# A scan's block inverse: a level works on 32 of 64 columns instead of all

## The chip, the cores and the metric

The kernel runs on one core of one Trainium2 chip. The metric is the device time of one execution in microseconds (us); lower is better. A change is judged by the median of several runs beside runs of the kernel before.

## The reference, cut to what matters

The program is four transformer layers in sequence (two of one model, two of another), 256 tokens by 1024 channels in f32. The second layer mixes tokens by a recurrence over time for each of 16 heads of 64 channels:

```
def step(state, inp):
    r_t, w_t, k_t, v_t, a_t, b_t = inp
    sa = jnp.einsum('bhij,bhj->bhi', state, a_t)
    state = (state * w_t[:, :, None, :] + sa[..., None] * b_t[:, :, None, :]
             + v_t[..., None] * k_t[:, :, None, :])
    y_t = jnp.einsum('bhij,bhj->bhi', state, r_t)
    return state, y_t
```

All else in the layers (feed-forward nets, attentions, norms) is not touched by the change.

## The kernel before

The recurrence is computed in chunks of 64 tokens. Within a chunk the terms `sa` depend on one another through a strictly triangular 64x64 matrix L, so that each head and chunk needs the inverse of a unit triangular matrix. It is built by doubling. At level lv the matrix consists of diagonal blocks of b = 2^lv tokens whose inverses are already there; two neighbouring blocks make a pair, and the level fills in the corner that joins them: (inverse of one) x (corner of L) x (inverse of the other). Levels 1 to 5 take b from 2 to 32 up to the whole 64.

A tile of 128 tokens is t (0 or 1). It holds two chunks (e = 0, 1), which lie on the two halves of the partitions. The 16 heads are two groups o (0, 1) of eight, each group four pairs r of two heads x. So `sY[o]` is [128, 4, 2, 64]: partitions (e, token), then r, x, and 64 columns. There are 2 tiles x 2 groups x 5 levels = 20 level steps, and each of them is this work:

- `level_a` on TensorE: four transposes of `sY` (L2311, called X below), and sixteen 64x64 products W = L x Y (L2317), on the four quarters of the array in turn (`UNITS`).
- ScalarE copies the transposes from PSUM to `sX` (L2446); VectorE copies W from PSUM to `sW` (L2504, 512 columns).
- `level_b` on TensorE: sixteen 64x64 products Y = X x W (L2328). It waits for both copies.
- VectorE writes the new corner into `sY` by a copy under a mask (L2510, 512 columns); the mask `rMK[:, 4 + lv, :]` is bf16, read as uint16 and repeated over r and x. The next level's transposes wait for it.

Each f32 product shows as two MATMUL and two LDWEIGHTS records in the trace, so the 320 products of L2317 and of L2328 are 640 records each.

The order of the work is written out by hand in `scan_steps()`, and every engine follows that one list, each in its own queue. For t = 0 a level is: level_a of o = 0, level_a of o = 1, a small product `scl` (L2259, levels 1 to 4), level_b of o = 0, level_b of o = 1, then `complete` (levels 0 to 4), which is work for the other tile: up to level 2 only on VectorE, from level 3 also on TensorE (L1785), ScalarE and VectorE (L2094 to L2099). At levels 4 and 5 `tt` (transposes L2270 for the other tile, with a copy L2497) follows. For t = 1 a level is the two level_a and the two level_b, and beside them: `state` (L2376, L2385) after level 1, `yo` (L2400 to L2412) after level 2, and pieces of `norm`, a normalisation of the scan's output on VectorE with a part on ScalarE (L2474) and on GpSimd (L964, L966): its first three pieces after level 3, the rest of that half and three of the next after level 4, the rest after level 5. What follows the scan is the layer's output product (L490 to L492) and a norm.

Of the kernel before, what the change touches and what calls it, by code (L numbers as in the profile page):

```python
# [7 lines left out]
F32 = mybir.dt.float32  # L8
# [6 lines left out]
P = 128  # L15
# [12 lines left out]
HD = 64  # L28
# [212 lines left out]
class Net:  # L241


    def __init__(self, nc, A, out, ctx, stages):
# [6 lines left out]
        def at(name, offset, shape, dt):  # L251
            return nc.alloc_sbuf_tensor_at(name, shape, dt, offset=BASE + offset)

        o = 0
# [16 lines left out]
        XO = o  # L271
# [67 lines left out]
        self.TT01 = [at(f"sTA{t}", (TO + 8192, EO + 24576)[t], [P, 8, 2, P], F32) for t in range(T)]  # L339
        self.TT23 = [at(f"sTB{o}", XO + 4096 * o, [P, 4, 2, P], F32) for o in range(2)]  # L340
        self.sX = [at(f"sXX{o}", XO + 8192 + 4096 * o, [P, 4, P], F32) for o in range(2)]
        self.sW = [at(f"sWW{o}", XO + 10240 + 4096 * o, [P, 2, 4, HD], F32) for o in range(2)]
        self.KR0 = [at(f"sKR{o}", XO + 8192 + 4096 * o, [P, 4, 2, HD], F32) for o in range(2)]
        self.KR1 = [[at(f"sKQ{t}{o}", spot, [P, 4, 2, HD], F32) for o, spot in enumerate(spots)] for t, spots in
                    enumerate(((second + 4096, second + 6144), (AO + 4096, JO)))]
# [1959 lines left out]
    def pe_scan_level_a(self, pe, t, o, lv):  # L2305
        L, Y = self.sL[o], self.sY[o]
        bank, _ = self.scan_pair(pe, ("x", t, o, lv), (self.moved, "x", t, o, lv))
        pe.wait_ge(self.made, "y", t, o, lv - 1)
        pe.wait_ge(self.made, "l", t, o)
        for r in range(4):  # L2310
            m = pe.e.transpose(bank[:, r * P:(r + 1) * P], Y[:, r, :, :].rearrange("p x n -> p (x n)"), self.ident[:, :])  # L2311
        m.then_inc(*self.product.up("x", t, o, lv))
        banks = self.scan_pair(pe, ("w", t, o, lv), (self.made, "w", t, o, lv))
        for r in range(4):
            for e, x in self.UNITS:
                h = self.HALF[e]
                m = pe.e.matmul(banks[e][self.HALF[x], r * HD:(r + 1) * HD], L[h, r, x, :], Y[h, r, x, :], start=True,  # L2317
                                stop=True)
        m.then_inc(*self.product.up("w", t, o, lv))

    def pe_scan_level_b(self, pe, t, o, lv):
        banks = self.scan_pair(pe, ("y", t, o, lv), (self.made, "y", t, o, lv))
        pe.wait_ge(self.moved, "x", t, o, lv)
        pe.wait_ge(self.made, "w", t, o, lv)
        for r in range(4):
            for e, x in self.UNITS:
                h = self.HALF[x]
                m = pe.e.matmul(banks[x][self.HALF[e], r * HD:(r + 1) * HD], self.sX[o][h, r, e * HD:(e + 1) * HD],  # L2328
                                self.sW[o][h, e, r, :], start=True, stop=True)
        m.then_inc(*self.product.up("y", t, o, lv))  # L2330

# [159 lines left out]
    def dve_rwkv_scan(self, dve, n):  # L2491
        dve.wait_ge(self.d_one["masks"])
        for kind, *a in self.scan_steps() + list(self.SCAN_TAIL):
            if kind == "tt":
                t, o = a
                dve.wait_ge(self.product, "tt", t, o, 1)
                dve.e.tensor_copy(self.TT23[o][:, :, :, :].rearrange("p r i n -> p i r n"), self.scan_banks(  # L2497
                    "tt", t, o, 1).rearrange("p (i r n) -> p i r n", i=2, r=4)).then_inc(*self.made.up("tt", t, o))
            elif kind == "gram":
                self.dve_scan_gram(dve, *a)  # L2500
            elif kind == "level_a":
                t, o, lv = a
                dve.wait_ge(self.product, "w", t, o, lv)
                dve.e.tensor_copy(self.sW[o][:, :, :, :], self.scan_banks("w", t, o, lv).rearrange(  # L2504
                    "p (e c) -> p e c", e=2)[:, :, 0:256].rearrange("p e (r n) -> p e r n", r=4)).then_inc(
                    *self.made.up("w", t, o, lv))
            elif kind == "level_b":
                t, o, lv = a
                dve.wait_ge(self.product, "y", t, o, lv)
                dve.e.copy_predicated(self.sY[o][:, :, :, :].rearrange("p r x n -> p x r n"), self.scan_mask(4 + lv, True),  # L2510
                                      self.scan_banks("y", t, o, lv).rearrange("p (x c) -> p x c", x=2)[
                                          :, :, 0:256].rearrange("p x (r n) -> p x r n", r=4)).then_inc(
                    *self.made.up("y", t, o, lv))
            elif kind == "seen":
                c, = a
                t, h = c // 2, self.HALF[c % 2]
                for o in range(2):
                    x = self.sA[t][h, 4 * o:4 * o + 4, :, :].rearrange("p r x n -> p x r n")
                    banks = self.scan_banks("seen", c, 0 if c == 3 else o)
                    dve.wait_ge(self.product, "seen", c, 1 if c == 3 else o)  # L2520
                    dve.wait_ge(self.moved, "sa0", t, o, 1)
                    dve.e.tensor_tensor(x, banks[h, :].rearrange("p (x r n) -> p x r n", x=2, r=8)[
                        :, :, 4 * o:4 * o + 4, :], x, ALU.add).then_inc(*self.made.up("sa", c, o))
            elif kind == "state":
                self.dve_scan_state(dve, *a)
            elif kind == "complete":
                self.dve_scan_complete(dve, *a)
            elif kind == "norm":
                t, h, first, end = a
                for seg in range(first, end):  # L2530
                    self.dve_scan_norm(dve, t, h, seg)
            elif kind == "turn":
                t, q = a
                hi, lo = (x[:, 4 * q:4 * q + 4, t * P:(t + 1) * P] for x in (self.XH, self.XL))
                dve.wait_ge(self.moved, "ro", t, q)
                dve.e.tensor_tensor(lo, self.bank(self.place["turn", ("ro", t, q)]).rearrange("p (k s) -> p k s", k=4),
                                    hi.bitcast(F32), ALU.subtract).then_inc(*self.made.up("ro", t, q))
        self.dve_out(dve, n)

    def scan_mask(self, i, bits=False):  # L2540
        m = self.rMK[:, i, :].bitcast(mybir.dt.uint16) if bits else self.rMK[:, i, :]
        return m.unsqueeze(1).unsqueeze(1).broadcast_to([P, 2, 4, HD])
# [238 lines left out]
```

## Time and profile before

| | |
|---|---|
| three timed runs | 2408.38, 2408.85, 2411.97 us; median 2408.85 |
| the profiled execution | 2401.35 us, of which the span is 2399.5 us |
| TensorE busy in the span | 2278.4 us (95%) |
| VectorE busy | 1493.5 us (62%) |
| ScalarE busy | 1158.4 us (48%) |
| mean granted TensorE clock | 0.983 |

PE is TensorE's matmuls, PEld its weight loads, DVE VectorE, ACT ScalarE, POOL GpSimd. The profiled execution was 7.5 us faster than the median of the timed ones, so durations are taken from its trace and differences are set against the median. The levels of the scan lie between 911.5 and 993 us of the span.

### The profile page before, as it was taken

The numbers are of one execution on the slowest core, as the hardware profiler recorded it, in microseconds if no ns is written. First come the engines' busy times: TensorE is split into PE (matmuls) and PEld (weight loads), VectorE is DVE, ScalarE is ACT, GpSimd is POOL, SyncE is SP. The second block draws the span as 40 slices with busy tenths as digits, with TensorE's granted clock in tenths as the row PEclk, the third lists the DMA queues.
The fourth block names the chain that finished last, engine by engine and source line by source line (L and its number), as shares of the span: only waits on it lengthen the run. The fifth ranks groups of instructions, "written<-read, shape, count | busy, mean of one in ns | idle before, by whom it ended". The sixth has DMA issues, their size and how long they took to land.

```text
span 2399.5 us, 32778 instructions
## 1 busy us (share of the span) xinstructions
PE 2278.4 (95%) x12883; PEld 1840.0 (77%) x12883; DVE 1493.5 (62%) x2069; ACT 1158.4 (48%) x1672; POOL 175.0 (7%) x288
## 2 busy tenths in 40 slices
PE   8999999999998988889999999998999999969998
PEld 6888778887887557768887888866888788748886
DVE  5656657647665867576557656655655765647655
ACT  5445545446544453244455445444445544545444
POOL 1001000001000010410011000001000000041001
PEclk9999999999999999989999999999999999989999
DMA  7556636554646420056555655513555555506552
GB/s 243 191 182 216 216 122 220 180 192 156 213 165 213 156 99 4 21 179 193 177 200 167 192 185 197 178 36 116 188 184 193 176 186 185 194 10 205 177 184 105
DMA packets 289751, 395.68 MB, mean 165 GB/s; under 512 B 11672, under 2 KB 193248, under 8 KB 289600
## 3 DMA queue, kind: packets, MB, share of 16 engines
q1 hardware_dynamic: 284800, 377.33, 47.4%
q0 software_dynamic: 4656, 16.20, 2.0%
q8 instruction: 104, 1.70, 0.3%
q14 instruction: 47, 0.39, 0.0%
q10 hardware_dynamic: 144, 0.07, 0.0%
HBM read 392.50 MB, written 1.05 MB: 164 GB/s over the span
## 4 chain that ended last, share of the span: by engine, by line
PE 75%; DVE 6%; ACT 4%; issue 2%; POOL 1%; DMA 0%; DVEq 0%; POOLq 0%; ACTq 0%; SPq 0%
PE bank L490 22%; PE bank L492 22%; PE bank L491 22%; PE bank L516 1%; PE bank L1320 1%; ACT wh L605 1%; PE bank L504 1%; ACT JUNK L612 1%; DVE wl L789 1%; DVE TMP L827 1%; DVE qPS L1677 0%; DVE H L847 0%; PE bank L1322 0%; PE bank L1347 0%; PE bank L1334 0%
## 5 line engine op out<-in xcount | busy, mean ns | idle before, releaser
L789 DVE TENSOR_TENSOR wl<-raw,wh 128x1024 fp32r<-128x1024 f32 x708 | 859.4, 1224 | 592.0 <-ACT wh L605 591.1
L605 ACT ACTIVATE wh<-raw 128x1024 fp32r<-128x1024 f32 x708 | 743.9, 1058 | 671.3 <-PE bank L492 641.7
L490 PE MATMUL bank<-wh,XH 128*128 128x512 f32 x2000 | 802.6, 401 | 26.8 <-DVE XL L806 6.1
L491 PE MATMUL bank<-wl,XH 128*128 128x512 f32 x2000 | 784.5, 392 | 0.0
L492 PE MATMUL bank<-wh,XL 128*128 128x512 f32 x2000 | 784.3, 392 | 0.0
L490 PEld LDWEIGHTS bank<-wh,XH 128*128 128x128 f32 x2000 | 379.1, 190 | 116.2 <-issue 20.5
L492 PEld LDWEIGHTS bank<-wh,XL 128*128 128x128 f32 x2000 | 378.6, 189 | 82.2
L491 PEld LDWEIGHTS bank<-wl,XH 128*128 128x128 f32 x2000 | 379.7, 190 | 74.4 <-issue 0.5
L490 PE MATMUL bank<-wh,AH 128*128 128x512 f32 x704 | 276.0, 392 | 0.0
L492 PE MATMUL bank<-wh,AL 128*128 128x512 f32 x704 | 274.1, 389 | 0.0
L491 PE MATMUL bank<-wl,AH 128*128 128x512 f32 x704 | 274.1, 389 | 0.0
L492 PEld LDWEIGHTS bank<-wh,AL 128*128 128x128 f32 x704 | 132.1, 188 | 27.9
L491 PEld LDWEIGHTS bank<-wl,AH 128*128 128x128 f32 x704 | 132.2, 188 | 26.8
L490 PEld LDWEIGHTS bank<-wh,AH 128*128 128x128 f32 x704 | 132.2, 188 | 26.6
L987 POOL TENSOR_SCALAR ST<-ST 128x1 f32<-128x1 f32 x32 | 8.3, 259 | 1359.2 <-ACT JUNK L612 1358.8
L702 ACT ACTIVATE AH<-bank 128x512 fp32r<-128x512 f32 x88 | 52.7, 599 | 111.8 <-PE bank L516 111.6
L891 DVE TENSOR_TENSOR AL<-bank,AH 128x512 fp32r<-128x512 f32 x88 | 60.8, 691 | 56.4 <-ACT AH L702 56.4
L921 DVE SCALAR_TENSOR_TENSOR att<-att,ST,bank 128x256 f32<-128x256 f32 x176 | 84.7, 481 | 6.2
L617 ACT ACTIVATE XH<-CT 128x512 fp32r<-128x512 f32 x60 | 37.3, 629 | 101.6 <-DVE CT L800 101.6
L732 ACT ACTIVATE att<-bank,ST 128x256 f32<-128x256 f32 x176 | 72.3, 462 | 12.7 <-POOL ST L1020 12.7
L918 DVE SCALAR_TENSOR_TENSOR att<-att,bank 128x256 f32<-128x256 f32 x176 | 72.9, 414 | 5.2 <-ACT att L732 5.2
L847 DVE SCALAR_TENSOR_TENSOR H<-TMP,ST,H 128x512 f32<-128x512 f32 x64 | 45.3, 749 | 24.5 <-POOL ST L991 24.5
(317 smaller groups left out, 1771.0 us busy)
## 6 DMA issues: line engine op xcount, KB each, us to landing
raw<-in_ffn_w_dram SPq DMA_DIRECT2D x184, 512.0 KB, 4.6
raw<-in_ffn_wi_dram SPq DMA_DIRECT2D x176, 512.0 KB, 4.6
raw<-in_ffn_w_dram SPq DMA_DIRECT2D x40, 1024.0 KB, 4.9
raw<-in_ffn_wo_dram SPq DMA_DIRECT2D x40, 1024.0 KB, 4.9
raw<-in_a_wqkv_dram SPq DMA_DIRECT2D x18, 1024.0 KB, 4.8
raw<-in_a_w_in_dram SPq DMA_DIRECT2D x16, 1024.0 KB, 5.7
raw<-in_b_w_in_dram SPq DMA_DIRECT2D x12, 1024.0 KB, 4.9
bc<-in_norm_g_dram POOLq DMA_DIRECT2D x16, 512.0 KB, 5.4
```

What stands on the lines that cost most here:

```text
L490: pe.e.matmul(o, a, h, start=(k == 0), stop=False)
L491: pe.e.matmul(o, a, l, start=False, stop=False)
L492: m = pe.e.matmul(o, b, h, start=False, stop=(k == layer.nk - 1))
L605: act.e.activation(self.wh[j % N_W][:, 0:p.size], self.raw[p.chunk % N_RAW][:, p.at:p.at + p.size], ACT.Copy).then_inc(*self.rounded.up(j))
L617: act.e.activation(self.XH[:, 4 * b:4 * b + 4, t * P:(t + 1) * P], self.CT[b][:, :, :], ACT.Copy).then_inc(*self.x_hi.up(n, t, b))
L702: act.e.activation(self.AH[:, 2 * b:2 * b + 2, :], bank.rearrange("p (k s) -> p k s", k=2), ACT.Copy).then_inc(*self.hid_hi.up(n, b))
L732: act.e.activation(self.att[b % 3][:, t * FB:(t + 1) * FB], self.pair((n, "up", b))[t][:, 0:FB], ACT.Tanh, scale=sc[:, t:t + 1]).then_inc( ...
L789: dve.e.tensor_tensor(self.wl[j % N_W][:, 0:p.size], self.raw[p.chunk % N_RAW][:, p.at:p.at + p.size], self.wh[j % N_W][:, 0:p.size].bitca ...
L847: dve.e.scalar_tensor_tensor(part, self.TMP[:, t, b, 512:1024], x, part, ALU.mult, ALU.add).then_inc(*self.resid.up(n, t, b))
L891: dve.e.tensor_tensor(lo, bank.rearrange("p (k s) -> p k s", k=2), hi.bitcast(F32), ALU.subtract).then_inc(*self.hid_lo.up(n, b))
L918: dve.e.scalar_tensor_tensor(x, x, 1.0, pair[:, 0:FB], ALU.add, ALU.mult).then_inc(*self.gate.up(n, b, t))
L921: dve.e.scalar_tensor_tensor(x, x, sc[:, T + t:T + t + 1], pair[:, FB:2 * FB], ALU.mult, ALU.mult).then_inc(*self.gated.up(n, b, t))
```

## The change

For a level only the second block of each pair has new columns: 32 of the 64 columns of each head, at every level. The kernel after multiplies and moves only those.

- W: the product's moving side is the second blocks' columns of Y, picked by a strided view (`scan_right`, runs of b columns every 2b); the result is 32 packed columns a unit.
- The copy of W to `sW` moves 256 columns in place of 512.
- Y = X x W has 32 moving columns in place of 64. The weights (`sX`, `L`) and their loads stay at 64 columns.
- The copy under the mask moves 2 x 128 columns in place of 512. It becomes two instructions, one for each x, with a view of `sY` in runs of b columns; only the second of them signals.

```
-        self.sW = [at(f"sWW{o}", XO + 10240 + 4096 * o, [P, 2, 4, HD], F32) for o in range(2)]
+        self.sW = [at(f"sWW{o}", XO + 10240 + 4096 * o, [P, 2, 4, 32], F32) for o in range(2)]
...
-                m = pe.e.matmul(banks[e][self.HALF[x], r * HD:(r + 1) * HD], L[h, r, x, :], Y[h, r, x, :], start=True,
-                                stop=True)
+                m = pe.e.matmul(banks[e][self.HALF[x], r * 32:(r + 1) * 32].rearrange("p (g b) -> p g b", b=2 ** lv),
+                                L[h, r, x, :], self.scan_right(Y[h, r, x, :], lv), start=True, stop=True)
...
-                m = pe.e.matmul(banks[x][self.HALF[e], r * HD:(r + 1) * HD], self.sX[o][h, r, e * HD:(e + 1) * HD],
+                m = pe.e.matmul(banks[x][self.HALF[e], r * 32:(r + 1) * 32], self.sX[o][h, r, e * HD:(e + 1) * HD],
                                 self.sW[o][h, e, r, :], start=True, stop=True)
...
-                dve.e.tensor_copy(self.sW[o][:, :, :, :], self.scan_banks("w", t, o, lv).rearrange(
-                    "p (e c) -> p e c", e=2)[:, :, 0:256].rearrange("p e (r n) -> p e r n", r=4)).then_inc(
-                    *self.made.up("w", t, o, lv))
+                dve.e.tensor_copy(self.sW[o][:, :, :, :].rearrange("p e r n -> p e (r n)"), self.scan_banks(
+                    "w", t, o, lv).rearrange("p (e c) -> p e c", e=2)[:, :, 0:128]).then_inc(*self.made.up("w", t, o, lv))
...
-                dve.e.copy_predicated(self.sY[o][:, :, :, :].rearrange("p r x n -> p x r n"), self.scan_mask(4 + lv, True),
-                                      self.scan_banks("y", t, o, lv).rearrange("p (x c) -> p x c", x=2)[
-                                          :, :, 0:256].rearrange("p x (r n) -> p x r n", r=4)).then_inc(
-                    *self.made.up("y", t, o, lv))
+                b = 2 ** lv
+                mask = self.scan_right(self.rMK[:, 4 + lv, :].bitcast(mybir.dt.uint16), lv)
+                for x in range(2):
+                    m = dve.e.copy_predicated(
+                        self.sY[o][:, :, x, :].rearrange("p r (g i b) -> p r g i b", i=2, b=b)[:, :, :, 1, :],
+                        mask.unsqueeze(1).broadcast_to([P, 4, 32 // b, b]),
+                        self.scan_banks("y", t, o, lv)[:, x * 512:x * 512 + 128].rearrange("p (r g b) -> p r g b", r=4, b=b))
+                m.then_inc(*self.made.up("y", t, o, lv))
...
+    def scan_right(self, x, lv):
+
+        return x.rearrange("p (g i b) -> p g i b", i=2, b=2 ** lv)[:, :, 1, :]
```

## Rows read from the trace of the kernel before

**Rows 1.** The page's first part: busy time, share of the span, instructions.

```profile
PE 2278.4 (95%) x12883; PEld 1840.0 (77%) x12883; DVE 1493.5 (62%) x2069; ACT 1158.4 (48%) x1672; POOL 175.0 (7%) x288
```

**Rows 2.** Busy time by stretch: both tiles' levels; granted clock, DMA share, GB/s last.

```profile
911.50:938.00 26.50, 25.68 (x660) 20.77 (x659) 22.47 (x34) 11.59 (x23) 0.00 (x0) 1.00 0.01 3
...
956.00:992.00 36.00, 26.47 (x906) 23.27 (x904) 21.71 (x36) 8.15 (x15) 11.64 (x10) 0.93 0.01 3
```

**Rows 3.** Groups by line and shape: busy us, mean ns, idle before and its releaser.

```profile
L2510 DVE COPY_PREDICATED sYY<-rMK,bank 128x512 f32<-128x512 uint16 x20 | 14.1, 728 | 4.1 <-PE bank L2328 3.9
L2317 PE MATMUL bank<-sYY,sLL 64*64 64x64 f32 x640 | 13.9, 224 | 0.1
...
L2328 PE MATMUL bank<-sWW,sXX 64*64 64x64 f32 x640 | 13.5, 231 | 9.4 <-DVE sWW L2504 9.4
L2504 DVE COPY sWW<-bank 128x512 f32<-128x512 f32 x20 | 13.3, 685 | 7.9 <-PE bank L2317 7.8
```

**Rows 4.** Timeline, level 2 of tile 0: start, duration, engine, line, idle and releaser.

```profile
916.52 0.66 PE L2311 MATMUL bank<-ident,sYY 128*128 128x128 f32 x4 [0.39 <-DVE sYY L2510]
...
918.95 1.05 PE L2259 MATMUL bank<-rCU,rLW 128*128 128x2 f32 x8
...
919.02 1.28 DVE L2504 COPY sWW<-bank 128x512 f32<-128x512 f32 x2
...
919.93 1.21 PE L2328 MATMUL bank<-sWW,sXX 64*64 64x64 f32 x64
...
920.69 1.34 DVE L2510 COPY_PREDICATED sYY<-rMK,bank 128x512 f32<-128x512 uint16 x2 [0.39 <-PE bank L2328]
...
921.48 0.66 PE L2311 MATMUL bank<-ident,sYY 128*128 128x128 f32 x4 [0.34 <-DVE sYY L2510]
```

**Rows 5.** Timeline: group 1 at level 5 of tile 0, level 1 of tile 1.

```profile
938.53 0.69 DVE L2504 COPY sWW<-bank 128x512 f32<-128x512 f32 x1 [0.22 <-PE bank L2317]
...
958.57 0.69 DVE L2504 COPY sWW<-bank 128x512 f32<-128x512 f32 x1 [0.52 <-PE bank L2317]
...
959.40 0.69 PE L2328 MATMUL bank<-sWW,sXX 64*64 64x64 f32 x32 [0.44 <-DVE sWW L2504]
```

**Rows 6.** Timeline, tile 1: end of level 3, level 4, and level 5.

```profile
976.00 0.74 DVE L2510 COPY_PREDICATED sYY<-rMK,bank 128x512 f32<-128x512 uint16 x1 [0.26 <-PE bank L2328]
...
979.61 1.28 DVE L2504 COPY sWW<-bank 128x512 f32<-128x512 f32 x2
...
980.43 1.29 PE L2328 MATMUL bank<-sWW,sXX 64*64 64x64 f32 x64 [2.07 <-DVE sWW L2504]
981.19 1.34 DVE L2510 COPY_PREDICATED sYY<-rMK,bank 128x512 f32<-128x512 uint16 x2 [0.30 <-PE bank L2328]
...
982.43 0.67 DVE L2619 TENSOR_REDUCE rSM<-rK 128x8 f32<-128x512 f32 x1
...
990.31 1.98 PE L2328 MATMUL bank<-sWW,sXX 64*64 64x64 f32 x64 [5.85 <-DVE sWW L2504]
```

**Rows 7.** VectorE work of other sizes: ns min/median/max.

```profile
L1267 DVE TENSOR_TENSOR dTR<-TMP,dRP x48: 216/219/226, 1478.2 to 1535.0; 128x64 f32<-128x64 f32 x48
...
L2577 DVE TENSOR_TENSOR sSS<-bank,sSS x4: 410/420/424, 962.0 to 1002.6; 128x256 f32<-128x256 f32 x4
```

**Rows 8.** Products of other widths: durations (ns min/median/max), then two runs of them.

```profile
L2317 PE MATMUL bank<-sYY,sLL x640: 218/218/268, 912.2 to 984.2; 64*64 64x64 f32 x160
...
L2290 PE MATMUL bank<-sTA,sTB x256: 269/269/418, 898.2 to 952.5; 64*64 64x128 f32 x128
...
L2259 PE MATMUL bank<-rCU,rLW x32: 251/251/272, 914.0 to 931.0; 128*128 128x2 f32 x32
...
907.39 1.96 PE L2290 MATMUL bank<-sTA,sTB 64*64 64x128 f32 x64
...
917.11 0.69 PE L2317 MATMUL bank<-sYY,sLL 64*64 64x64 f32 x32
```

**Rows 9.** Two single microseconds: busy time of each engine, clock, DMA.

```profile
979.00:980.00 1.00, 0.00 (x0) 0.00 (x0) 1.00 (x2) 0.86 (x2) 0.00 (x0) 1.00 0.00 0
...
988.00:989.00 1.00, 0.00 (x0) 0.00 (x0) 0.23 (x2) 0.86 (x2) 0.00 (x0) 0.50 0.00 0
```

## The prediction

> **What bounds the kernel now.** I read the page first. TensorE is busy 95% of the span and no other engine over 62% [rows 1], so for the kernel as a whole the products are the bound. That average says nothing of the scan, which is a different stage, so the next view was busy time by stretch. While the levels of tile 0 run, TensorE is nearly full (25.68 of 26.5 us); while those of tile 1 run it has 26.47 of 36 us, so something else sets a quarter of that time. DMA share is 0.01 in both: no transfer matters here [rows 2]. The groups by line then give the most that the change could touch: 13.9 + 13.5 us of products, 13.3 us of copies of W and 14.1 us of copies under the mask, all told 55 us, or 2% of the span. Their idle columns say which of it is waited for: TensorE sat idle 9.4 us for the copy of W [rows 3], and how much of that belongs to the copy itself has to be read in the order of time. The chain of waits and the timeline of each level show three kinds of level:
>
> - Tile 0, levels 1 and 2: TensorE runs X, W, X, W, `scl`, Y, Y without a break, then X of the next level stands idle 0.39 and 0.34 us for the copy under the mask of group 0. The copy of W is hidden: it begins at 919.02 and takes 0.69 us, and Y begins only at 919.93, when `scl` leaves TensorE [rows 4]. At levels 3 and 4 TensorE goes on with other products after Y, and nothing waits for either copy.
> - Tile 0 level 5 and tile 1 levels 1 to 3: nothing stands between W and Y of group 1. The copy of W of group 1 starts as W ends and Y starts as the copy ends (958.57 + 0.69, then 959.40) [rows 5].
> - Tile 1 from the end of level 3: VectorE is the chain. Copy under the mask, norm pieces, both copies of W, (Y on TensorE), both copies under the mask, next norm piece at once [rows 6]. TensorE waits 2.07 us there and 5.85 us at level 5.
>
> So the change shortens a chain in 2 + 4 levels and in the two and a bit at the end; in the other places of the 20 steps it shortens work that nobody waits for.
>
> **The products.** Half the moving columns does not mean half the time. 64 records of 128 columns span 1.96 us, (1.96 - 0.27) / 63 = 27 ns apart; with four quarters in turn, that is 107 ns a quarter. 32 records of 64 columns span 0.69: (0.69 - 0.22) / 31 = 15.2 ns, 61 ns a quarter, not the 54 that half of 107 would be. The records of `scl` have only 2 moving columns but 128 columns of weights: 8 in 1.05 us, (1.05 - 0.25) / 7 = 114 ns apart [rows 4, 8]. So spacing there is the weight load's; half of 114 for 64 columns of weights is 57, which is what the 61 nearly is. The change leaves the weights at 64 columns. I therefore take the spacing as unchanged, and count only the last record's own duration: 269 ns at 128 columns and 218 at 64, 51 less for 64 columns [rows 8], so 26 ns less for 32. Bounds: nothing, if a strided read costs what the skipped columns would; and spacing halved to 7.6 ns, 31 x 7.6 = 0.24 us a group of 32, if the stream is what counts after all.
>
> The Trainium skill, "TensorE: Matmul & The Clock Gate", section "LDWEIGHTS (loading the stationary operand)", says that a weight load takes its column count over 1.2 GHz, whatever the rows; the same page's "Back-to-back issue gap" gives a stream of moving columns at 2.4 GHz. By the first 64 columns of weights are 53 ns and no product gets shorter, by the second alone each would, which is the rival priced below.
>
> **The copy of W.** 512 columns take 685 ns [rows 3]; no copy of 256 stands in this stretch, but a VectorE operation from PSUM on 256 takes 420 [rows 7]. That is 265 less, 1.03 ns a column. On the line through both, 64 columns would take 221, and the trace has 219 for 64, in runs of eight columns at that [rows 7], so the fixed part is 155 and short runs cost nothing extra there. I take 0.265 us off each copy.
>
> **The copy under the mask.** One of 512 takes 728 ns; two in a row take 1.34 us, so the second starts 0.61 after the first [rows 3, 4], and they overlap by 0.12. One of 128 columns is then 728 - 384 x 1.03 = 0.33 us. The pair, with the same overlap, is 0.21 + 0.33 = 0.54 in place of 0.73: 0.19 us off. No row shows a copy under a mask of this size or with runs of 2 columns. Bounds: each of the two as long as the one before, +0.61 us; or only 0.07 off, if they don't overlap at all. The value I take lies by the line of rows 7, which holds down to 64 columns.
>
> The rule that speaks against this part is in the Trainium skill, "VectorE: DVE Perf Modes", section "The TRN2 errata — SBUF-src ops pay a fixed extra latency per instruction": the fixed cost comes once per instruction, and operations under 512 elements are to be avoided. By its fitted form (N + 151) / 0.96 the pair in sequence is 0.58 us, and the sum below would be 0.2 us smaller.
>
> **The sum.**
> - Tile 0, levels 1 and 2: 0.19 for the pair + 0.026 for Y, twice: 0.43. TensorE's idle of 0.34 or more covers it [rows 4].
> - Tile 0 level 5, tile 1 levels 1 to 3: 0.265 + 0.026 for the end of W, four times: 1.16.
> - End of tile 1's level 3: norm starts after the second pair, 0.19 + 0.026 sooner: 0.22.
> - Levels 4 and 5 of tile 1: the first copy of W 0.265, Y 0.026, the second pair 0.19; the second copy of W is off the path, since Y of group 1 comes 0.6 us after Y of group 0; and the second pair can't start sooner than its product, so the first pair's gain goes there. 0.48, twice: 0.96.
>
> Together 2.8 us. Levels 1 to 4 of the copies in tile 0, and levels 3 and 4 of its masks, are at nothing: `scl` and L1785 hide them, and the slack only grows, as VectorE gets some 9 us of the 27.4 us of these copies back (20 x 0.265 + 20 x 0.19). Nothing after the scan has a due time of its own (DMA 0.01, raw weights long there), so what the scan gives is passed on. The execution of this trace would be 2401.35 - 2.8 = 2398.6; set against the median of the timed runs, 2408.85 - 2.8 = 2406.0. That is 0.12%, under the 0.2% (4.8 us) that a measurement of this kernel can tell from no change.
>
> **Rivals.**
> - *The stream counts.* The products do take half. Some 30 groups of 32 records stand on TensorE's chain (all in tile 0 but the covered ones, about 17; three a level in levels 1 to 3 of tile 1; a few after): 30 x 0.24 = 7.3 us more, 2398.7. For it: 61 is not 57. Against it: 114 ns with two moving columns.
> - *The clock falls.* Slower. Half as many columns pass through the array in the same time. TensorE's clock is granted by what it did: after stretches without a product at 979 to 980 it was still at full (2.4 GHz), after the longer idle from 984.5 on it was at 0.50 (1.2 GHz) by 988, and the two Y groups that ran there took 1.98 us in place of 1.29 [rows 6, 9], 26 ns apart in place of 15. If the sparser products in tile 0's levels count as idleness, the 14 us of them that are groups of W and Y grow by that factor of 1.7, 9.8 us: 2415.8. It decides from 4 us of such work at the lower clock, which eat up the 2.8. Against it: `scl` with 2 columns runs at full clock now, and the spacing of instructions stays. (The page on TensorE, section "What's actually happening", has activity release the throttle; it doesn't say that half-wide products fail to.)
> - *The short pair is dear.* If runs of 2 to 16 columns or the second instruction cost what a full one does, +0.61 in place of -0.19 at the seven places where a pair stands in a chain (two in tile 0, one, two, two in tile 1), of which the sum has five: 7 x 0.61 = 4.3, less the copies' 1.6: 2411.5.
> - *It is hidden.* Another wait ends last in the chains (ScalarE's `sX`, the small GpSimd steps): 2408.5.
>
> **How the numbers follow.** The forecast 0.62; stream 0.12; clock 0.10; dear pair 0.08; hidden 0.08. Of the forecast's cases 0.10 are measured faster by over 0.2%, since it is over half way there and the timed runs alone differ by 3.6 us; 0.02 slower. Faster: 0.10 + 0.12 = 0.22. Slower: 0.02 + 0.08 of the clock + 0.03 of the pair = 0.13. Same: 0.65. The range goes from the stream rival, 2399, to somewhat over the dear pair, 2413, and leaves the deep clock case out. The forecast's own range is 2403 to 2409.
>
> **What the profile after would show.** L2504 on 256 columns at 0.42 us; L2510 x40 at 0.33, pairs 0.54 long; L2317 and L2328 with 32 columns, 192 ns each, a group still 0.67 long; idle before X at level 2 of tile 0 down to about 0.2; Y of tile 1's level 1 0.29 sooner after W; clock as before. Groups of 32 products in 0.45 us would prove the stream rival, a granted clock under 1 between 911 and 985 the clock rival, a pair over 0.73 us the dear one.

## The result

The changed kernel is a little faster: 2404.66 us median of 20 runs (2398.92 to 2411.9), the kernel before 2411.26 us (2403.49 to 2416.49, 20 runs). The ratio is 0.9976 with a 95% interval of 0.9966 to 0.9985, so 5.8 us less (3.6 to 8.2); the ratio is not that of the two medians, which lie 6.6 us apart. Later sessions gave the same kernel 0.9980 (0.9961 to 0.9999) and 0.9982 (0.9968 to 0.9997). The forecast was 2.8 us less, called "same", and the range 2399 to 2413. The median lies in the range; the timed size is larger than forecast and, in this first session, just on the other side of the line of 0.2%. The sign holds, and so does where the time was gained; one term of the sum had the wrong cause (below, the products).

The profiled execution after took 2406.57 us, that of before 2401.35. Single executions scatter by more than the effect, so a comparison of the two spans would say "slower". What the change did has to be read in the stage it touches.

The groups by line, of the kernel after (L2510 became L2512):

```profile
L2317 PE MATMUL bank<-sYY,sLL 64*64 64x32 f32 x640 | 13.4, 222 | 0.1
...
L2328 PE MATMUL bank<-sWW,sXX 64*64 64x32 f32 x640 | 12.9, 227 | 7.8 <-DVE sWW L2504 7.8
...
L2512 DVE COPY_PREDICATED sYY<-rMK,bank 128x128 f32<-128x128 uint16 x40 | 10.6, 329 | 7.1 <-PE bank L2328 6.8
...
L2504 DVE COPY sWW<-bank 128x256 f32<-128x256 f32 x20 | 8.0, 419 | 9.3 <-PE bank L2317 9.3
```

Beside [rows 3]: the products fell from 13.9 + 13.5 us to 13.4 + 12.9 with half the columns, the copy of W from 685 to 419 ns, and the copy under the mask from 728 to 329 ns, of which there are now twice as many. TensorE's idle time for the copy of W fell from 9.4 to 7.8 us. The two copies' lines together are busy 18.6 us in place of 27.4.

The timeline of levels 1 and 2 of tile 0, which answers to [rows 4]:

```profile
926.26 1.30 DVE L2512 COPY_PREDICATED sYY<-rMK,bank 128x128 f32<-128x128 uint16 x4 [1.16 <-PE bank L2328]
927.04 0.65 PE L2311 MATMUL bank<-ident,sYY 128*128 128x128 f32 x4 [0.38 <-DVE sYY L2512]
...
930.39 1.13 PE L2328 MATMUL bank<-sWW,sXX 64*64 64x32 f32 x64
...
931.13 0.96 DVE L2512 COPY_PREDICATED sYY<-rMK,bank 128x128 f32<-128x128 uint16 x4 [0.94 <-PE bank L2328]
931.67 0.66 PE L2311 MATMUL bank<-ident,sYY 128*128 128x128 f32 x4
```

After level 1 the first pair takes 0.72 us from 926.26 on, and X still stands idle 0.38 us; after level 2 the pair takes 0.50 us and X starts 0.15 us after Y's end (930.39 + 1.13, then 931.67), where before there was 0.34. X waits for the pair there too, only less. The two levels differ in the width of the runs: 2 columns at level 1, 4 at level 2. The durations (ns min/median/max) of the four copies of each level:

```profile
L2512 DVE COPY_PREDICATED sYY<-rMK,bank x4: 441/478/481, 926.3 to 927.1; 128x128 f32<-128x128 uint16 x4
...
L2512 DVE COPY_PREDICATED sYY<-rMK,bank x4: 284/292/301, 931.1 to 931.8; 128x128 f32<-128x128 uint16 x4
```

In tile 1, where nothing covers the copy of W ([rows 5]), Y now starts 0.57 us after the copy does, in place of 0.83:

```profile
968.17 0.42 DVE L2504 COPY sWW<-bank 128x256 f32<-128x256 f32 x1 [0.76 <-PE bank L2317]
...
968.74 0.67 PE L2328 MATMUL bank<-sWW,sXX 64*64 64x32 f32 x32 [0.17 <-DVE sWW L2504]
```

The products' own records, of all levels in the kernel after (ns min/median/max):

```profile
L2317 PE MATMUL bank<-sYY,sLL x640: 219/219/241, 922.8 to 992.1; 64*64 64x32 f32 x160
```

With 64 columns the median was 218 ns [rows 8]. So a record did not get shorter with half its columns (192 was forecast); what changed is how far apart the records start.

Laid out by the starts of X (L2311), counted from the first of them, the trace gives a measure that repeats to 0.02 us within tile 0, far finer than the timed runs:

| us from one X to the next | before | after | forecast gain | gain |
|---|---|---|---|---|
| tile 0, level 1 to 2 | 4.95 | 4.87 | 0.22 | 0.08 |
| tile 0, level 2 to 3 | 4.96 | 4.63 | 0.22 | 0.33 |
| tile 0, level 3 to 5 | 14.37 | 14.17 | 0 | 0.20 |
| tile 0 level 5 to tile 1 level 1 | 20.16 | 19.82 | 0.29 | 0.34 |
| tile 1, level 1 to 2 | 6.49 | 6.18 | 0.29 | 0.31 |
| tile 1, level 2 to 3 | 9.35 | 9.03 | 0.29 | 0.32 |
| tile 1, level 3 to 4 | 4.02 | 3.67 | 0.29 | 0.35 |
| tile 1, level 4 to 5 | 6.10 | 5.35 | 0.70 | 0.75 |
| from there to the last start of L2400 | 27.4 | 26.8 | 0.48 | 0.7 |
| sum, "the stage" below | 97.8 | 94.5 | 2.8 | 3.3 |

The expectations below have 94.4 and 3.4 for the last row, from starts read to a tenth of a microsecond.

### The profile page after: what moved, and what is told of

Same layout as the page of the kernel before. It is cut to its first block, busy times and chain, and to the rows that moved or that the text cites. A ratio compares the mean times of both kernels' runs of the same rounds, so it can differ in the third digit from the quotient of the medians.

```text
span 2404.8 us, 32798 instructions
## 1 busy us (share of the span) xinstructions
PE 2284.5 (95%) x12883; PEld 1843.5 (77%) x12883; DVE 1485.4 (62%) x2089; ACT 1158.4 (48%) x1672; POOL 174.6 (7%) x288
## 4 chain that ended last, share of the span: by engine, by line
PE 76%; DVE 6%; ACT 3%; issue 2%; POOL 1%; DMA 0%; DVEq 0%; POOLq 0%; ACTq 0%
PE bank L490 22%; PE bank L492 22%; PE bank L491 22%; PE bank L516 1%; PE bank L1320 1%; PE bank L504 1%; DVE wl L789 1%; ACT JUNK L612 1%; ACT wh L605 1%; DVE TMP L827 1%; DVE H L847 0%; PE bank L1347 0%; PE bank L1322 0%; PE bank L1334 0%; DVE qPS L1677 0%
## 5 line engine op out<-in xcount | busy, mean ns | idle before, releaser
L504 PE MATMUL bank<-ident,H 128*128 128x128 f32 x240 | 40.5, 297 | 22.2 <-DVE H L847 16.9
```

The source lines that it names most:

```text
L504: m = pe.e.transpose(bank[:, i * P:(i + 1) * P], self.H[:, t, k * P:(k + 1) * P], self.ident[:, :])
```

## The experiments

Three questions were open: why the timed effect is larger than the stage shows, what the parts of the change give, and what sets the time of the narrow products and of the short copies.

**The two kernels again.** No edit; each timed against the kernel before.

> The kernel before, unchanged, timed against itself. Stage length is read in the trace from the first X (L2311) to the last start of L2400: 97.8 us in the trace of before, 94.4 in that of after. Theory 1 (the whole effect lies in the scan's levels and the rest of the timed 5.8 us is scatter of the parts outside): the stage comes out at 97.8 within 1 us again, and the ratio within 0.998 to 1.002. Theory 2 (the stage itself scatters by some us, so that 3.4 us between two traces says little): a stage length more than 1.5 us off 97.8.

> The changed kernel, unchanged. Theory 1: stage 94.4 us within 1 us, total 3 to 4 us less than before within the scatter. Theory 2: another stage length by over 1.5 us. Theory 3 (the change also gives something outside of the stage, about 2.4 us): the stage repeats, and from the last L2400 to the end of the span the trace is 2 us or more shorter than in the kernel before, again.

Measured: the kernel before against itself came out at 1.0015, with an interval of 1.0002 to 1.0028. Two sets of runs of one and the same kernel differ by 3.6 us, so the edge of an interval can't be trusted to better than some 0.15%. The changed kernel gave 0.9980. All instructions of X and of L2400 in the second trace of before, and then in that of after (ns min/median/max, first and last start):

```profile
L2311 PE MATMUL bank<-ident,sYY x80: 272/273/474, 916.9 to 989.9; 128*128 128x128 f32 x80
...
L2400 PE MATMUL bank<-sSS,sTA x96: 217/219/267, 971.9 to 1016.9; 64*64 64x64 f32 x96
```

```profile
L2311 PE MATMUL bank<-ident,sYY x80: 272/273/477, 913.6 to 984.7; 128*128 128x128 f32 x80
...
L2400 PE MATMUL bank<-sSS,sTA x96: 217/219/267, 967.5 to 1010.1; 64*64 64x64 f32 x96
```

1016.9 - 916.9 is 100.0 us, and 1010.1 - 913.6 is 96.5, where the first traces had 97.8 and 94.5. So theory 2 is right: the stage scatters by some 2.1 us within each kernel. First trace against first, the kernels differ by 3.3 us, second against second by 3.5; but crossed, the pairs give 1.3 and 5.5, so these two differences agree partly by luck. What repeats is finer. Up to level 5 of tile 0 the two traces of each kernel agree to 0.02 us. Between there and level 5 of tile 1 the two of before differ by 0.05, 0.07 and 0.44 us (20.15 and 20.21; 6.50 and 6.57; 6.10 and 6.54, and the last has the clock at half in it), and the two of after at one place: 20.48 in place of 19.82 us between level 5 of tile 0 and level 1 of tile 1. There TensorE stops for 0.32 us in the middle of L2347, with nothing that the profile shows to wait for:

```profile
948.21 0.50 PE L2347 MATMUL bank<-sSA,sYY 64*64 64x64 f32 x10 [0.32 <-issue]
```

The masked copy alone (next) has such a stop at the same line, of 0.22 us, and 20.48 us there too, against 20.15 and 20.21 of before. So the gain of 0.34 us at that place stands only between traces without the stop. What scatters behind the first X of level 5 in tile 1 is mostly the clock (below).

**The masked copy alone, and all but the masked copy.**

```
-                dve.e.copy_predicated(self.sY[o][:, :, :, :].rearrange("p r x n -> p x r n"), self.scan_mask(4 + lv, True), ...
+                for x in range(2):
+                    m = dve.e.copy_predicated(
+                        self.sY[o][:, :, x, :].rearrange("p r (g i b) -> p r g i b", i=2, b=b)[:, :, :, 1, :],
...
+                        self.scan_banks("y", t, o, lv)[:, x * 512:x * 512 + 256].rearrange(
+                            "p (r g i b) -> p r g i b", r=4, i=2, b=b)[:, :, :, 1, :])
```

> The kernel before with the masked copy alone changed: two instructions of 128 columns that read the second blocks out of the 64-column products; products and copy of W as before. At blocks of 4 and more the pair takes 0.50 us in place of 0.73, at blocks of 2 it takes 0.73 as before. Theory 1: 0.23 off at four places that stand in the chain (tile 0 level 2; tile 1 end of level 3, level 4, level 5): stage 97.8 - 0.9 = 96.9 us. Rival (the pair is what gives most of the 3.4): stage under 96 us.

The other kernel is the changed one with the product's target strided and the old masked copy:

```
+                m = pe.e.matmul(self.scan_right(banks[x][self.HALF[e], r * HD:(r + 1) * HD], lv),
+                                self.sX[o][h, r, e * HD:(e + 1) * HD],
+                                self.sW[o][h, e, r, :].rearrange("p (g b) -> p g b", b=2 ** lv), start=True, stop=True)
```

> The changed kernel with the masked copy alone undone: one instruction of 512 columns, into whose bank the narrow products of Y now write their 32 columns at their own places. Theory 1: stage 94.4 + 0.9 = 95.3 us. Rival (the pair gives most): stage over 96.5 us. If the scattered write of the products costs something, the groups of L2328 are over 0.67 us long.

Measured, in the part that repeats (first X to the first X of level 5 in tile 0): 24.28 us before, 23.98 with the pair alone, 23.91 with all but the pair, 23.67 with both. The pair gives 0.30 and 0.24, the rest 0.37 and 0.31. The whole stage was 98.0 and 97.0 us, over the 96.9 and 95.3 expected: the clock was at half for 10 and 14 us of it where the first traces had 7 us, and the pair alone took 0.3 us longer than before where its stop at L2347 lies. So the whole stage doesn't test how the gain divides; the part that repeats does. The timed ratios, 1.0001 (0.9986 to 1.0016) and 1.0009 (0.9991 to 1.0028), show neither of the parts faster, though each is by the trace; all but the pair even has a median of 2413.90 us beside the 2409.31 of before. The scattered write of the products costs nothing: a mean record of L2328 takes 228 ns there and 227 here.

**The products alone undone**, twice.

```
+                m = pe.e.matmul(banks[e][self.HALF[x], r * HD:(r + 1) * HD].rearrange("p (i g b) -> p g i b", i=2, b=2 ** lv),
+                                L[h, r, x, :], Y[h, r, x, :].rearrange("p (g i b) -> p g i b", i=2, b=2 ** lv),
+                                start=True, stop=True)
...
+                m = pe.e.matmul(banks[x][self.HALF[e], r * HD:(r + 1) * HD].rearrange("p (i n) -> p i n", i=2),
+                                self.sX[o][h, r, e * HD:(e + 1) * HD],
+                                self.sW[o][h, e, r, :].unsqueeze(1).broadcast_to([HD, 2, 32]), start=True, stop=True)
```

> The changed kernel with the products alone undone: 64 moving columns again (W over all 64 columns of Y, its output order chosen so that the 32 new ones lie together; Y over sW's 32 columns read twice), copies of 256 and 2 x 128 as in the changed kernel. Theory A (spacing is set by the weight load, as forecast): a group of 32 records goes from 0.67 back to 0.69 us and the next product starts 0.02 later. From the first X to the first X of level 5 of tile 0 the trace takes 24.28 us before and 23.67 after; here about 23.67 + 17 x 0.02 = 24.0. Rival (the stream counts): over 24.3.

Measured: 23.98 us to level 5 of tile 0 (24.0 expected), and 68.37 to level 5 of tile 1 (68.32 in the second run of it, reported under the clock) where the changed kernel has 67.72 and the kernel before 70.40. So of the 2.68 us gained up to there the narrow products give 0.60 to 0.65, and the narrow copies the other 2.0. Its ratio is 0.9990 (0.9976 to 1.0004).

**Half the weights.** The rows 32 to 63 of each product are left out, so this kernel computes something else; it is for the timing alone.

```
+                q = slice(64 * x, 64 * x + 32)
+                m = pe.e.matmul(banks[e][q, r * 32:(r + 1) * 32].rearrange("p (g b) -> p g b", b=2 ** lv),
+                                L[h, r, x, 0:32], self.scan_right(Y[h, r, x, :], lv), start=True, stop=True)
...
+                q = slice(64 * e, 64 * e + 32)
+                m = pe.e.matmul(banks[x][q, r * 32:(r + 1) * 32], self.sX[o][h, r, e * HD:e * HD + 32],
```

> The changed kernel with 32 columns of weights in each product of W and Y in place of 64: half of the rows of W and of Y are left out. Theory A (the weight load sets the spacing: 57 to 61 ns a quarter of the array, 14.5 apart with four in turn): the groups' records come about half as far apart, 7 to 8 ns, and a group of 32 takes 0.45 us in place of 0.67. Theory B (14.5 ns is what the engine needs to issue a record, whatever its size): still 0.67 us.

The timeline, level 2 of tile 0, the changed kernel's group first, then the one with half the weights:

```profile
927.62 0.67 PE L2317 MATMUL bank<-sYY,sLL 64*64 64x32 f32 x32
```

```profile
920.75 0.46 PE L2318 MATMUL bank<-sYY,sLL 64*32 64x32 f32 x32
```

0.46 us, as theory A has it. Half the moving columns took a group from 0.69 to 0.67, half the weights on top from 0.67 to 0.46. (0.67 - 0.22) / 31 = 14.5 ns, 58 a quarter of the array; with 0.19 us for the last record (0.46 - 0.19) / 31 = 8.7 ns, 35 a quarter. From the first X to the first X of level 5 of tile 0 it takes 20.96 us in place of 23.67. The Trainium skill, "TensorE: Matmul & The Clock Gate", section "LDWEIGHTS (loading the stationary operand)", counts 53 and 27 ns for 64 and 32 columns of weights; the runs agree with the rule and lie 5 to 8 ns above.

**Which side of the short runs costs.**

```
-                mask = self.scan_right(self.rMK[:, 4 + lv, :].bitcast(mybir.dt.uint16), lv)
+                mask = self.rMK[:, 4 + lv, 0:32].bitcast(mybir.dt.uint16).rearrange("p (g b) -> p g b", b=b)
```

> The changed kernel, but the masked copy reads its mask as 32 columns in a row (of the wrong columns, so what it copies differs); target and source as they are. At level 1 (runs of 2 columns) one of these copies took 0.47 us, at the other levels 0.29. Theory M (the uint16 mask in runs of 2 is what costs): level 1 falls to 0.29 us too. Theory T (the f32 target in runs of 2 costs): stays at 0.47. The first X to the second level's X: 4.87 us, under M 4.63 as at level 2.

```
-                        self.sY[o][:, :, x, :].rearrange("p r (g i b) -> p r g i b", i=2, b=b)[:, :, :, 1, :],
+                        self.sY[o][:, :, x, 32:64].rearrange("p r (g b) -> p r g b", b=b),
```

> The changed kernel, but the masked copy writes 32 columns in a row (not where they belong); mask and source as they are. Theory M: level 1 stays at 0.47 us. Theory T: it falls to 0.29.

All forty copies of each (ns min/median/max), first with the mask in a row, then with the target in a row:

```profile
L2512 DVE COPY_PREDICATED sYY<-rMK,bank x40: 282/294/492, 925.0 to 998.9; 128x128 f32<-128x128 uint16 x40
```

```profile
L2512 DVE COPY_PREDICATED sYY<-rMK,bank x40: 289/298/303, 919.3 to 992.9; 128x128 f32<-128x128 uint16 x40
```

The maximum of 492 ns stays with the flat mask (the four of level 1 in tile 0 have a median of 480), and X of level 2 still comes at 4.87 us. With the flat target it is gone, and X of level 2 comes at 4.64 us. Theory T: it is the f32 target in runs of two.

**A version beyond the change.** From level 2 on one masked copy of 256 columns for the pair:

```
+                if lv > 1:
+                    dve.e.copy_predicated(
+                        self.sY[o][:, :, :, :].rearrange("p r x (g i b) -> p (r x) g i b", i=2, b=b)[:, :, :, 1, :],
+                        mask.unsqueeze(1).broadcast_to([P, 8, 32 // b, b]),
```

> The changed kernel, but from level 2 on the masked copy is one instruction of 256 columns (heads and pairs merged into one dimension of the target). By the line of the VectorE rows 256 columns take 0.46 us in place of the pair's 0.50, so 0.04 off at about six places: X of level 3 in tile 0 9.46 after the first X in place of 9.50, the whole some 0.2 us, not to be told in the timed runs. Rival (a fourth dimension in the pattern costs): over 0.50 us.

and with it, at level 5, where the rows of the first block lie together, half the weights for W and half the rows for Y:

```
+                q, n = (slice(64 * x, 64 * x + 32), 32) if lv == 5 else (self.HALF[x], HD)
...
+                                L[h, r, x, 0:n], self.scan_right(Y[h, r, x, :], lv), start=True, stop=True)
```

> one_mask, and at level 5 the products of W load 32 columns of weights in place of 64 (the rows of the first block are all that Y needs), and Y contracts over those 32 rows. Result as before. By the run with 32 columns of weights a W group falls from 0.67 to 0.46: of the four at level 5 the two of tile 0 are in the chain, 0.4 us off between X of level 5 and the first L2339 of tile 0 (5.66 us in the changed kernel), one in part hidden by the copy. Rival: tiles of 32 rows cost a switch, and Y's groups get longer than 0.67.

and the changed kernel a third time, beside them:

> The changed kernel, unchanged, once more, on the chip of the two runs below. Theory 1 (the effect is the 3.4 us of the stage, the rest of the timed 5.8 us is what the ratio scatters between sessions, as the kernel before against itself came out at 1.0015): ratio 0.9986 within 0.0015, first X to last L2400 94.4 us plus at most 2.2 for the clock. Theory 3 (some 2.4 us more outside of the stage): ratio 0.9976 again, and from the last L2400 to the end of the span 1388.5 us or less (1388.2 and 1385.6 in the two traces of it, 1390.1 and 1392.7 in those of before).

The one copy takes 0.43 us in place of the pair's 0.50:

```profile
L2512 DVE COPY_PREDICATED sYY<-rMK,bank x16: 427/434/445, 928.9 to 997.4; 128x256 f32<-128x256 uint16 x16
```

X of level 5 in tile 1 comes at 67.72 us in the changed kernel, 67.55 with one copy, 67.35 with the lighter level 5 as well; the W groups of that level take 0.46 us at the full clock. By the trace each step is a gain, of 0.2 us; the timed ratios are 0.9982 (0.9968 to 0.9997), 0.9974 (0.9959 to 0.9989) and 0.9975 (0.9960 to 0.9989), which do not part the three. Both are faster than the kernel before; that they beat the changed one is read from the stage alone. At level 5 of tile 0 X to the first L2339 takes 5.51 us in place of 5.71 (the 5.66 of the expectation is misread). That is 0.20 gained, less than the 0.4 expected: the second W group waits 0.34 us for a copy of tile 1's transposes (L2500), so only one group's gain counts. The rival is not borne out: with 32 rows a Y group there is still 0.67 us long.

Theory 3 is not borne out by the trace: behind the stage the third trace has 1393.4 us, and the other two 1388.2 and 1385.6, against 1390.1 and 1392.7 of before. Three traces against two can't exclude a small effect there.

**The clock.** The last run was for this.

> The changed kernel with products of 64 moving columns once more, for the clock. In the traces so far the clock falls to half once or twice between 68 and 87 us after the first X, where TensorE idles for the norm. With 64 columns (4 traces) it was at half for 6.8, 6.8, 10.2 and 10.2 us, and where it fell at the first idle it came back at 73, under X and W of level 5; with 32 columns (7 traces up to target_flat, one_mask and trim) five show one stretch of about 14 us, through X and W of level 5. Theory C (half as many columns don't bring the clock back there): here again no stretch over 7 us in one piece. Theory S (only where in time the idle happens to lie decides): a stretch of 14 us can come here too.

Busy time by stretch, granted clock third from the end, of the changed kernel (third trace) and of the kernel before (second trace), about the end of tile 1:

```profile
988.00:990.00 2.00, 1.90 (x36) 1.43 (x35) 0.71 (x2) 0.00 (x0) 1.23 (x1) 0.50 0.00 0
990.00:994.50 4.50, 0.36 (x15) 0.39 (x17) 3.49 (x7) 1.60 (x3) 0.00 (x0) 0.50 0.00 0
994.50:997.50 3.00, 3.00 (x107) 3.00 (x104) 1.57 (x5) 0.46 (x1) 0.20 (x1) 0.50 0.02 5
```

```profile
987.50:989.00 1.50, 1.50 (x24) 1.00 (x19) 1.37 (x3) 0.00 (x0) 0.00 (x0) 0.50 0.05 11
989.00:993.50 4.50, 1.84 (x68) 1.46 (x68) 2.37 (x5) 0.00 (x0) 1.85 (x2) 1.00 0.00 0
```

In both TensorE had idled for the norm before, and level 4's Y or level 5's X and W ran at 0.50 (1.2 GHz). In the kernel before the clock was back at 1.00 by 989; in the one after it stayed at 0.50 through X and W of level 5, the next idle and level 5's Y, 14 us in all. Counted over the traces: with 64 moving columns (both of before, the pair alone, the wide products twice) the clock was at half for 6.8, 10.2, 10.2, 6.8 and again 6.8 us, never over 7.5 in one piece; with 32 (nine traces, all kernels with narrow products) six have one piece of 14 us and three one of about 7, among them the one with half the weights, whose clock fell early, at 68.4 us, and was back at 75.2.

The last run fits theory C, but says little: in it, as in two others with 64 columns, the clock fell only at 75 us, so that there was no earlier fall to recover from. Just two traces with 64 columns had the early fall, and they differ from the six in more than the columns. Their copies of W were wide as well, and X of level 5 came at 70.7 and 71.0 us, some 2 us after the fall at 68.7; in the six it came at 67.4 to 68.6, within 1 us of the fall. So theory S, by which the place in time decides, explains the same traces, and nothing here parts the two. The kernel that would, narrow copies and wide products, was traced twice and had the early fall in neither. Which it is stays open.

What a long piece costs can be read behind the first X of level 5 in tile 1: 26.8 us with 7 us at half, 28.1 with 14, in both other traces of the changed kernel, so 1.3 us. The stage is 94.5 in the first case and 95.8 in the third trace; the second has 96.5, because it has the stop at L2347 besides.

## Why the prediction was right, and where it was off

- **Where the time is.** Right in the main: the uncovered levels gave most of it. The sum for the stage was 2.8 us and the trace has 3.3; the means of the three traces after and the two before are 3.3 apart as well. What was put at nothing, tile 0 from level 3 to 5, gave 0.20 us. Most of it is the products', each group of which got shorter there too: that part takes 14.32 us with wide products and narrow copies, 14.17 with both narrow.
- **The copy of W.** Right to a hundredth: 0.265 off a copy forecast, 0.266 measured (685 to 419 ns), and 0.31 to 0.35 where it is uncovered, 0.02 to 0.06 more than the 0.29, which is the products' part.
- **The masked copy.** Right but for level 1. A short one takes 0.29 us, not 0.33, and the pair 0.50, not 0.54: 0.24 off in place of 0.19. At level 1 it takes 0.47, the pair 0.73, nothing gained, where 0.19 was counted. That is the direction of the dear-pair rival, at a fraction of its price: it had each copy as long as the full one, a pair of 1.34 us. Rows of runs of eight columns didn't reach down to two.
- **The products.** That the weight load sets the time was right, and the stream rival, 7.3 us, is refuted by the groups of 0.67 us and by the run with half the weights. The term of the sum was wrong in its cause. It held the spacing unchanged and took 0.026 us off the last record's own duration. The record kept its 218 ns (219), and the spacing fell from 15.2 to 14.5 ns, 58 a quarter, which is what `scl`'s 57 had promised: 31 x 0.7 = 0.02 us a group, near the 0.026 by chance. Since a shorter spacing shortens each group in the chain, and not the nine ends that the sum counts (0.23), it came to 0.60 to 0.65 us by the runs with wide products. That is the term that was mis-sized. (The 7.3 should read 7.2, 30 x 0.24.)
- **The clock.** It never fell in tile 0's levels, or in tile 1's before 68 us after the first X, in any of the traces, so the rival is wrong for the levels that it named. Later on the clock stayed down for 14 us in six of nine traces with narrow products, at a price of 1.3 us in the changed kernel. That this is the rival's mechanism is not shown.
- **The total.** The timed difference is 5.8 us in the first session, 4.8 and 4.3 by the other ratios; the stage explains 3.3. Kernels with no difference come out 3.6 us apart, so the rest of 1.0 to 2.5 us lies within what the measurement makes by itself. Whether a part of it is real is open: the parts of the trace before and behind the stage scatter by 15 and 9 us from trace to trace. The chance of 0.65 for "same" rested on a bound of 0.2%, and the first measured ratio is at 0.24%: the same effect of 3.3 us (0.14%) can land on either side.

## What to carry to other kernels

Halving the moving columns of small products does little where the weight load sets their spacing; halve the weights' columns, and the group falls from 0.67 to 0.46 us. Copies out of PSUM do shrink with their columns, but only those with nothing beside them count: find them one by one in the timeline. An effect of a few us in 2400 is better read as distances between the same instructions in two traces, which repeat to 0.02 us where nothing stops TensorE and the clock is the same, than from timed runs that differ by 3.6 us for the same kernel.

## What the runs showed of the hardware

A copy under a mask on VectorE into an f32 target in runs of two columns takes 0.47 us for 128 columns, where runs of four to thirty-two take 0.29 and a target in a row takes 0.30; the uint16 mask in runs of two costs nothing. A product's strided source, strided target or a source read twice cost nothing that the trace shows. A product record with 64 columns of weights takes 218 ns with 64 moving columns and 219 with 32, and in a group of W the records start 15.2 and 14.5 ns apart. TensorE's clock, once at 1.2 GHz after an idle, came back at 72 us after the first X, under X and W of level 5, in the two traces with 64 moving columns that had the early fall; in six with 32, where X and W ran 2 to 4 us sooner, it stayed down until 82 us. Whether the columns or the time decide is open.
